# Left operands copied ahead of the weight splits, the first feed-forward stage in seven products per block, and the bias rows fetched at its end

## What is computed

```
def swiglu(h, w13, w2):
    g, u = jnp.split(h @ w13, 2, axis=-1)
    return ((jax.nn.silu(g) * u) @ w2).astype(h.dtype)
...
h = h + swiglu(rms_norm(h, norm_ffn[layer]), ffn_w13[layer], ffn_w2[layer])
```

## Time and profile before

| | |
|---|---|
| median of 3 runs | 1619.84 us (1617.91, 1619.84, 1623.19) |
| the profiled execution | 1617.46 us, span 1615.7 us |
| PE busy | 1599.0 us, 99% of the span |
| DVE busy / ACT busy | 1205.0 us (75%) / 867.8 us (54%) |
| granted TensorE clock | 1.0 throughout |
| stages, from the first turn of hid (us) | ffn0 167.72, ffn1 458.88, ffn2 642.16, ffn3 916.12, ffn4 1131.81, ffn5 1444.16 |

### The profile page before, as it was taken

One profiled execution on the slowest core, in us unless ns is written; L12 is line 12 of the kernel. 1 busy time (PEld: TensorE's weight loads), 2 busy tenths in 40 slices (PEclk: granted clock), 3 DMA queues, 4 the chain that ended last, 5 costly groups with the idle time before them and its releaser, 6 DMA issues.

```text
span 1615.7 us, 22339 instructions
## 1 busy us (share of the span) xinstructions
PE 1599.0 (99%) x9121; PEld 1377.3 (85%) x9121; DVE 1205.0 (75%) x1266; ACT 867.8 (54%) x1055; POOL 71.3 (4%) x83
## 2 busy tenths in 40 slices
PE   9999999999999999999999999999999999999999
PEld 7998888889888887888888888888888887788887
DVE  6687555575569997799887688986664577868996
ACT  6445554455555565555544556555443465855553
POOL 0233000000000000000000000000100002000000
PEclk9999999999999999999999999999999999999999
DMA  8535658564484725765464767347545662076641
GB/s 292 160 116 165 222 170 230 200 198 156 155 297 133 235 104 196 247 203 175 143 222 157 262 216 235 108 149 236 189 156 185 208 202 90 9 239 222 229 136 52
DMA packets 229686, 294.80 MB, mean 182 GB/s; under 512 B 7644, under 2 KB 185264, under 8 KB 229586
## 3 DMA queue, kind: packets, MB, share of 16 engines
q1 hardware_dynamic: 223978, 284.33, 53.1%
q10 hardware_dynamic: 5608, 9.06, 2.2%
HBM read 290.75 MB, written 1.57 MB: 181 GB/s over the span
## 4 chain that ended last, share of the span: by engine, by line
PE 77%; DVE 14%; DMA 3%; issue 3%; ACT 1%; SPq 1%; POOL 0%; DVEq 0%; POOLq 0%; ACTq 0%
PE ps L2507 20%; PE ps L2511 10%; PE ps L2676 10%; PE ps L2713 7%; DVE wlo L1583 3%; PE ps L2535 3%; PE ps L2546 3%; PE ps L2537 3%; PE ps L2498 2%; PE ps L2495 2%; PE ps L2496 2%; DVE wlo L1593 2%; DMA raw<-in_ffn_w_gate_up 2%; PE ps L2603 2%; PE ps L2605 2%
## 5 line engine op out<-in xcount | busy, mean ns | idle before, releaser
L1583 DVE TENSOR_TENSOR wlo<-raw,whi 128x2048 fp32r<-128x2048 f32 (+1 forms) x243 | 528.4, 2182 | 180.2 <-ACT whi L836 179.0
L2507 PE MATMUL ps<-x_both,whi 128*128 128x512 f32 x2080 | 496.7, 390 | 0.0
L836 ACT ACTIVATE whi<-raw 128x2048 fp32r<-128x2048 f32 x231 | 437.0, 1903 | 108.8 <-DMA raw<-in_ffn_w_gate_up 46.6
L2507 PEld LDWEIGHTS ps<-x_both,whi 128*128 128x128 f32 x2080 | 385.9, 188 | 77.2
L2511 PEld LDWEIGHTS ps<-x_both,wlo 128*128 128x128 f32 x2080 | 267.5, 191 | 10.6
L2511 PE MATMUL ps<-x_both,wlo 128*128 128x256 f32 x2080 | 270.7, 283 | 0.0
L1593 DVE TENSOR_TENSOR wlo<-arena,whi 128x2048 fp32r<-128x2048 f32 x56 | 127.9, 2284 | 5.5 <-ACT whi L849 5.5
L849 ACT ACTIVATE whi<-arena 128x2048 fp32r<-128x2048 f32 x56 | 107.4, 1918 | 31.4 <-DVE arena L1815 21.0
L2535 PE MATMUL ps<-whi,x_both 128*128 128x512 f32 x232 | 88.6, 392 | 0.1
L2495 PE MATMUL ps<-x_both,whi 128*128 128x256 f32 x352 | 88.4, 289 | 0.0
L2496 PE MATMUL ps<-x_both,wlo 128*128 128x256 f32 x352 | 86.2, 283 | 0.0
(11 more groups left out here) (336 smaller groups left out, 2376.5 us busy)
## 6 DMA issues: line engine op xcount, KB each, us to landing
raw<-in_ffn_w_gate_up SPq DMA_DIRECT2D x80, 1024.0 KB, 6.3
raw<-in_ffn_w SPq DMA_DIRECT2D x54, 1024.0 KB, 5.6
arena<-in_ffn_w_down SPq DMA_DIRECT2D x24, 1024.0 KB, 8.2
raw<-in_ffn_w_down SPq DMA_DIRECT2D x20, 1024.0 KB, 5.0
raw<-in_hgrn_w_in SPq DMA_DIRECT2D x14, 1024.0 KB, 5.6
raw<-in_moba_w_in SPq DMA_DIRECT2D x12, 1024.0 KB, 5.1
raw<-in_conv_w_in SPq DMA_DIRECT2D x10, 1024.0 KB, 5.1
arena<-in_ffn_w SPq DMA_DIRECT2D x8, 1024.0 KB, 7.9
```

The costliest lines, as they stand in the source:

```text
L836: act.activation(whi[s % WRING][:, 0:width], raw[chunks.slot(n)][:, 0:width], ACT.Copy).then_inc(split_hi, 1)
L1583: ins = dve.tensor_tensor(wlo[s % WRING][:, part], raw[chunks.slot(n)][:, part], whi[s % WRING][:, part].bitcast(F32), ALU.subtract)
L2507: pe.matmul(ps[:, bank + n, :], hi[:, k, n * P:(n + 1) * P], x_both[:, k], start=k == 0, stop=k == KT - 1, skip_group_check=True)
```

## The change

It has four parts.

1. In every blocked stage ACT and DVE make the left parts of a product ahead of the weight split of the same step, and the last product's ahead of the split of d8.
2. The left sum s4 is made in step p03 (p13) instead of p01 (p11), behind that step's split and ahead of its drain.
3. ffn0 goes from the standard to the blocked form.
4. The bias row is made in ffn0's step g3 (PSUM bank 2 instead of 7) and stored in step u3. Its 8 reads come at the stage's end, on ACT's queue between the splits of d10 and of moba's first chunk. `attention_parameters` follows the load of u1.

```
-BLOCKED = ["ffn1", "ffn2", "ffn3", "ffn5"]
+BLOCKED = ["ffn0", "ffn1", "ffn2", "ffn3", "ffn5"]
...
-LEFT_SUMS = {("g", 4): (0, (0, 1)), ("p", 0, 0): (0, (2,)), ("p", 0, 1): (0, (3,)),
-             ("g", 8): (1, (0, 1)), ("p", 1, 0): (1, (2,)), ("p", 1, 1): (1, (3,))}
+LEFT_SUMS = {("g", 4): (0, (0, 1)), ("p", 0, 0): (0, (2,)), ("p", 0, 3): (0, (3,)),
+             ("g", 8): (1, (0, 1)), ("p", 1, 0): (1, (2,)), ("p", 1, 3): (1, (3,))}
...   (SP, ffn: in the blocked form)
+                        if name == "ffn0" and i == 1:
+                            attention_parameters()
...   (ACT, ffn_blocked)
+                    if later[0] == "p":
+                        left_high(*later[1:])
                     split_item(ORDER[k + 3])
                     if k and before[0] == "g":
                         gate_silu(before[1])
-                    if later[0] == "p":
-                        left_high(*later[1:])
...
+                    if name == "ffn0" and item == ("u", 3):
+                        store_bias()
...
+                left_high(1, P_S4)
                 split(name, "d", STANDARD)
-                left_high(1, P_S4)
...
                 split(name, "d", STANDARD + 2)
+                if name == "ffn0":
+                    act.wait_ge(split_lo, product_split(first_block(name) + 1, P_A22) + 1)
+                    load_bias()
...   (DVE, ffn_blocked)
+                    if later[0] == "p":
+                        left_low(*later[1:])
                     split_item(ORDER[k + 3])
+                    if name == "ffn0" and item == ("g", 3):
+                        dve.wait_ge(bias_rowed, 1)
+                        dve.tensor_copy(bias_row, ps[0:HEADS, 2, :]).then_inc(bias_copied, 1)
                     if item in LEFT_SUMS:
                         b, sums = LEFT_SUMS[item]
                         for m in sums:
                             left_sum(b, m)
-                    if later[0] == "p":
-                        left_low(*later[1:])
...
+                left_low(1, P_S4)
                 split(name, "d", STANDARD)
-                left_low(1, P_S4)
...   (PE, ffn)
                 for item in ORDER[2:LAST_UP] if blocked else ():
+                    if name == "ffn0" and item == ("g", 3):
+                        pe.wait_ge(small_landed, 16 * 7)
+                        pe.matmul(ps[0:HEADS, 2, :], table[:], places, start=True, stop=True).then_inc(bias_rowed, 1)
+                    if name == "ffn0" and item == ("p", 0, P_A12):
+                        pe.wait_ge(bias_copied, 1)
```

More of the change, by code:

```diff
@@ L733, in ffn @@
                 load(down_rows(down, 0), name, "d", 0)
-                if name == "ffn0":
-                    attention_parameters()
                 for i in range(2, PAIRS):
@@ L1103, in ffn @@
                         activate(i)
[L1104 to L1107, removed]
                     if i == 1:
@@ L1758, in ffn_blocked @@
             def ffn_blocked(name):
-                alpha = 1.0 if name == "ffn1" else 0.5
+                alpha = 1.0 if name in ("ffn0", "ffn1") else 0.5
                 silus = FFNS.index(name) * (PAIRS + 1)
@@ L1946, in ffn @@
                     return
-                alpha = 1.0 if name == "ffn0" else 0.5
+                alpha = 0.5
                 base = parts_before(name)
@@ L2012, in ffn @@
                         keys_beside(i)
-                    if name == "ffn0" and i == 2:
-                        dve.wait_ge(bias_rowed, 1)
-                        dve.tensor_copy(bias_row, ps[0:HEADS, 7, :]).then_inc(bias_copied, 1)
                     if i < PAIRS - 2:
@@ L2768, in ffn @@
                         keys_beside(i)
-                    if name == "ffn0" and i == 2:
-                        pe.wait_ge(small_landed, 16 * 7)
-                        pe.matmul(ps[0:HEADS, 7, :], table[:], places, start=True, stop=True).then_inc(bias_rowed, 1)
                     down(0, i)
@@ L2774, in ffn @@
                     if i >= 1:
-                        if name == "ffn0" and i == 2:
-                            pe.wait_ge(bias_copied, 1)
                         if name == "ffn4" and i in (3, 4):
```

## The result

The kernel after takes 1609.03 us in the median of 4 runs (1608.15 to 1609.88); the kernel before, with one more run beside it, 1621.51 us (1617.91 to 1623.42). The ratio is 0.993, with a 95% interval of 0.9912 to 0.9949: faster by 0.7%, where 1611.9 us was forecast. The profiled executions lie 9.3 us apart (1617.46 and 1608.15 us). The ratio leans on few runs: two of the four executions of the kernel before are at 1623 us, and in the later sets beside the experiments its median is 1618.28 and 1618.57 us (17 runs each), 1618.88 us (9) and 1621.08 us (11). By these the change gives 9 to 12 us. Executions in a clearly slower state, such as one of 2249.73 us at a granted clock of 0.65, are left out of every median and ratio.

A forecast was written before the change was run, and what follows sets the result against it. PE was taken as the bound, busy 1599.0 of 1615.7 us. Order in the four old stages -4.2, ffn0 -4.4, bias reads +0.7: -7.9 from the median 1619.84 gives 1611.9 us; own range 1608 to 1615.5, with rivals 1605 to 1616.5.

The forecast's parts named there:

- Seven products in ffn0: In ffn0, 14 block products of 2.75 us replace eight pairs of down products of 5.46 us: -5.2 us.
- Left parts ahead of the split: In the four old blocked stages, PE's eight waits on DVE's left low part all go: -8.5 us.
- The drains: In ten blocks, s4 ahead of S2's drain makes product S3 late by 0.38 us each: +3.8 us.
- ffn2's backlog: In block 0 of ffn2, `final_norm` leaves DVE 1.3 us late, passed on to S2's drain: +1.3 us.
- Bias reads: At ffn0's end, their traffic delays the load of moba's second chunk: +0.7 us, between 0 and 3.9.
- The cover of 3.0 us: At moba's start, the second chunk may land late by 2.5 us ahead of ACT's split plus 0.5 us before PE's turn.
- The issues cost nothing: At ffn0's end, eight bias issues hold ACT 4.68 us, but it would wait for moba's chunk anyway: 0 us.
- the drain doesn't hold PE: Rival for the blocks: S3 does not wait for S2's drain; with free traffic too, 1606.1 us; chance 0.14.
- the new order does nothing: Rival for the blocked stages: DVE's sum of work is the bound and waits come back later; 1615.3 us, chance 0.09.
- The starved chunk: Rival at moba's start: the bias reads starve the second chunk, 3.9 us instead of 0.7; 1615.1 us, chance 0.15.
- DVE waiting for ACT: Rival in blocked stages: with left parts first, DVE waits each step for ACT's copy; slower, 1628.4 us, chance 0.05.
- the signs named: ffn0 near 169.3 us, L1797 waits gone, short drain waits in each block, moba's turn waiting under 1 us.

The follow-up runs named there:

- the last kernel: The kernel after with s4 back in p01 and p11, ffn2's final norm one step earlier, and the bias loads on SP's queue; ratio 0.9896 to before, median 1602.87 us.
- the order alone: The kernel before with only the moves of the left parts and of s4, ffn0 left in standard form; ratio 0.9969 to the kernel before.
- bias_late: The kernel after with the eight bias loads issued on ACT behind the work that opens moba; ratio 0.9948 to the kernel before.
- s4_twice: The kernel after with the sum s4 made twice in a row ahead of S2's drain; median 1618.07 us, ratio 0.9992 to the kernel before.
- all_three: The kernel after with s4 behind S2's drain, ffn2's final norm one step earlier and the bias loads late on ACT; ratio 0.9925 to the kernel before.
- before_again: The kernel before, unchanged, profiled once more; 1620.26 us, 2.8 us longer than its first profiled execution.

## Why the prediction was right

The direction, the mechanism and the range held. The forecast was -7.9 us between profiled executions; it is -9.3. That it comes so near is in part luck: ffn0's stretch gave 2.70 us where 3.7 were forecast, the four old blocked ones 4.85 where 4.2 were, and ffn4 and the part ahead of ffn0 gave 1.8 us that were in no term. By its steps:

- **Seven products in ffn0**, -5.2 us. Right. With two drains (0.7) and the turn's wait (1.6) the sum for the stage is -2.9 us; measured -2.70 to ffn1, and -2.87 within the stretch. In the last kernel, where none of these waits is left, the stretch is 5.4 us shorter.
- **Left parts ahead of the split**, -8.5 us. Right. The old blocked stages gave 4.85 us after 4.0 us had gone back to the drains, so the waits were worth 8.9; the last kernel, where the drains cost 0.2 us, shows 8.8 directly. The 0.23 us a wait beyond the idle time shown was needed: with 6.7 alone the sum misses by 2.
- **The drains**, 10 x 0.38 = +3.8 us. Measured 0.35 in each block (8.56 - 8.29, and 0.08 of restart). Between a drain's end and PE's start I had put 0.15 us; it is 0.10. Three experiments show the cause: s4 away from the drain takes the wait out, s4 twice adds s4's time.
- **ffn2's backlog**, +1.3 us beyond the ordinary drain. Measured 9.76 - 8.56 = 1.2, gone with the norm one step earlier.
- **Bias reads**, +0.7 us, the term that was mis-sized: it measured 1.6. The cover of 3.0 us was right; the lateness was not. The load took 10.1 us, 4.5 more than 5.6, and 4.5 - 3.0 = 1.5. I had put it near the lower bound because no other load stood ahead of it in its queue; that made it better than the 12.5 us of the earlier trace rows, by little. The bias reads' queue took 65.8% of the engines' time and the loads' 43.1% from 323.2 to 329.4 us (packets overlap, so the two add up to more than the whole). The Trainium skill (DMA: Bandwidth & Descriptors, section on queues, rings and completion order) says that each DMA engine goes round-robin between the queue rows, packet by packet; the trace agrees in so far as both queues went on moving data. The lateness of under 3 us and the term of 0 that I had worked out from it were too small: it was 4.5 us, between that and the 6.9 of the row.
- **"The issues cost nothing"** held where they stood and only there: moved behind the same splits they cost 2.4 us.
- **Not in the sum**: ffn4, -1.5 us; the work of no line changed there. This is as much as the profiled span fell beyond the forecast, and its cause stays open.
- **The median.** I took its distance from the profiled execution, 2.4 us, over to the kernel after, where it is 0.9. That is 1.5 us of the 2.9 by which the forecast is high; the other 1.4 are the sum's.

Of the rivals, "the drain doesn't hold PE" (1606.1 us) and "the new order does nothing" (1615.3 us) are ruled out by the spacing of S2 and S3 and by the order alone. The starved chunk was there at less than half its price. Of DVE waiting for ACT there is no sign: in the kernel after DVE never waits at the left part (L1798), and the stages got shorter. Of the signs named, two were missed: the turn waits 1.4 us and not under 1, and with it ffn0's stretch is 170.8 us and not near 169.3.

## What to carry to other kernels

An engine that feeds the bound one in order should make the small part that is wanted next ahead of the large one that is wanted later; what then stands ahead of a buffer's release counts too, as the sum here did in every block: it moves the drain by 0.60 us, 0.33 us were to spare (0.44 from the drain's end to S3's start, less the 0.10 that PE takes behind it), and S3 came 0.27 us late. Before an operation is moved along with others, ask whether it must be: s4's move cost 2 to 3 us and bought nothing. A DMA issue is work of the engine that issues it: put a group of them on a queue whose engine stands idle, and behind the loads that someone is about to wait for.

## What the runs showed of the hardware

- Behind an idle time of PE of 2.39 us (bias_late) and of 2.01 us (s4_twice) its clock fell to 1.2 GHz for 3.4 us: the granted clock is 0.51 and 0.50 over them, and matmuls follow each other at 0.43 us instead of 0.23.

```profile
349.00:351.20 2.20, 0.03 (x1) 0.06 (x1) 2.20 (x2) 2.20 (x2) 0.00 (x0) 1.00 1.13 203
...
351.40:354.80 3.40, 3.40 (x9) 2.62 (x9) 3.40 (x4) 0.90 (x1) 0.00 (x0) 0.51 1.11 240
...
354.90:358.60 3.70, 3.70 (x18) 3.04 (x17) 1.79 (x2) 0.98 (x1) 0.00 (x0) 1.00 1.10 348
```

  Behind 2.47 us in all_three it did not, nor behind the waits up to 1.4 us in any kernel. Half the clock over 3.4 us is 1.7 us of work; in s4_twice the product behind the wait takes 9.96 us to the next one instead of 8.38. But in bias_late little of it was a loss on top: all_three, at the full clock, waited 0.7 us for the next split instead, and ffn0's stretch is 4.1 us longer in it than in the last kernel (289.78 and 285.72 us), against the 4.3 us of bias_late.
- In three of 14 profiles (before_again, s4_twice, all_three) the clock fell in the same way in the attention, to 0.50 or 0.51 over 3.4 us, and the time grew by 1.5 to 1.7 us. The waits of 0.4 and 0.7 us ahead of it stand in all 14. The executions of the kernel before at 1617 to 1619 us have a mean clock of 0.999 or 1.0, most of those at 1620 to 1624 us one of 0.997 or 0.998. Such falls would fit that spread; only before_again, 1620.26 us at 0.999, shows one in a profile.
- The bias reads have small packets, 761 of them for 0.73 MB, beside 393 for 0.80 MB of the loads in the same 6.2 us: with fewer bytes they took half as much time again.

```profile
q10 hardware_dynamic: 761, 0.73, 65.8%
q1 hardware_dynamic: 393, 0.80, 43.1%
```
